# Modulation products spread through the projection steps' ring order in a two-block transformer kernel

## The reference

```python
c_act = jax.nn.silu(c)
for l in range(2):
    mod = c_act @ w_mod[l] + b_mod[l]            # 2048 x 6144
    shift, scale, gate = jnp.split(mod, 3, axis=-1)
    h = x * (1.0 + scale[:, None]) + shift[:, None]
    if l == 0:
        y = diff_attention(h, a_w_in, a_w_out, ...)
    else:
        mod_kv = c_act @ kv_w_mod + kv_b_mod      # 2048 x 4096
        k, v, F = shared_kv(x, ...)
        y = forgetting_attention(h, b_w_in, b_w_out, k, v, F)
    x = layer_norm(alpha * x + gate[:, None] * y, ln_g[l], ln_b[l])
# second block: adaln(c_2, w_mod_2) gives six vectors (2048 x 12288), then mixer, GLU, MLP
```

## Time and profile before

| what | value |
|---|---|
| median of 3 runs | 2741.72 us (2737.67 to 2751.97) |
| profiled execution, its own time | 2757.5 us |
| its span | 2755.6 us |
| PE busy | 2501.9 us, 91% |
| DVE busy | 1714.8 us, 62% |
| ACT busy | 1041.8 us, 38% |
| HBM traffic over the span | 255 GB/s |
| mean granted PE clock | 0.925 of full |

### The profile page before, as it was taken

How to read it: one execution, slowest core, us unless ns; L and a number is a source line. 1 busy time by engine, 2 the same in 40 slices (tenths; PEclk the granted TensorE clock), 3 DMA queues, 4 the chain that set the end, 5 groups by cost and what they waited for, 6 DMA issues and landing times.

```text
span 2755.6 us, 42740 instructions
## 1 busy us (share of the span) xinstructions
PE 2501.9 (91%) x18111; PEld 2059.6 (75%) x18111; DVE 1714.8 (62%) x2630; ACT 1041.8 (38%) x1556; POOL 177.4 (6%) x289
## 2 busy tenths in 40 slices
PE   5799999798789799989998958899899999999998
PEld 1588877566656598789854848578699898998986
DVE  4657789688767755356524755777755477655555
ACT  0253343344453333344423322344444444343443
POOL 1102233011100000111000000000000000000000
PEclk7799999899899899989977975999999999999999
DMA  9969999787678688969766748868645587755553
GB/s 353 337 219 356 349 336 313 234 294 288 244 260 308 244 286 308 353 209 312 258 220 218 249 90 309 327 232 276 236 133 189 183 274 276 244 184 191 188 171 107
DMA packets 317373, 699.74 MB, mean 254 GB/s; under 512 B 13600, under 2 KB 14080, under 8 KB 312192
## 3 DMA queue, kind: packets, MB, share of 16 engines
q1 hardware_dynamic: 298432, 627.27, 66.2%
q0 software_dynamic: 18480, 67.66, 7.0%
q10 hardware_dynamic: 272, 2.10, 0.2%
HBM read 646.77 MB, written 56.49 MB: 255 GB/s over the span
## 4 chain that ended last, share of the span: by engine, by line
PE 73%; DVE 15%; DMA 8%; ACT 2%; issue 1%; SPq 0%; POOL 0%; DVEq 0%; ACTq 0%; POOLq 0%
PE bank L2147 71%; DVE arena L1352 5%; DMA ring<-in_w_mod 3%; DMA ring<-in_a_w_in 3%; DVE ring_lo L1352 3%; DVE sm L1352 2%; DVE arena L1360 2%; PE bank L2150 1%; PE bank L2375 1%; DMA ring<-in_a_w_out 1%; DMA arena<-arena 0%; DVE MSB L1352 0%; DMA m_state<-MSB 0%; DVE LT L1360 0%; ACT att_w_hi L963 0%
## 5 line engine op out<-in xcount | busy, mean ns | idle before, releaser
L1352 DVE TENSOR_TENSOR ring_lo<-ring,w_hi 128x1024 fp32r<-128x1024 f32 (+1 forms) x380 | 427.7, 1134 | 359.9 <-ACT w_hi L963 334.8
L963 ACT CAST w_hi<-ring 128x1024 fp32r<-128x1024 f32 x316 | 330.6, 1049 | 472.5 <-PE bank L2147 470.4
L1352 DVE TENSOR_TENSOR ring_lo<-ring,att_w_hi 128x1024 fp32r<-128x1024 f32 x192 | 232.0, 1223 | 224.1 <-ACT att_w_hi L963 223.9
L963 ACT CAST att_w_hi<-ring 128x1024 fp32r<-128x1024 f32 x192 | 198.9, 1049 | 350.8 <-PE bank L2147 181.0
L2147 PE MATMUL bank<-in_hi,w_hi 128*128 128x256 f32 x1024 | 290.2, 283 | 1.2 <-DVE n L1357 1.2
L2147 PE MATMUL bank<-in_lo,w_hi 128*128 128x256 f32 x1024 | 290.1, 283 | 0.0
L2147 PE MATMUL bank<-in_hi,ring_lo 128*128 128x256 f32 x1024 | 289.7, 283 | 0.0
L2147 PE MATMUL bank<-w_hi,hid_lo 128*128 128x512 f32 x640 | 257.5, 402 | 5.2 <-DVE ring_lo L1352 5.2
L2147 PE MATMUL bank<-ring,cpad 128*32 128x512 f32 x1408 | 195.7, 691 | 26.1 <-DMA ring<-in_w_mod 22.5
L2147 PE MATMUL bank<-att_w_hi,att_hi 128*128 128x512 f32 x512 | 206.0, 402 | 6.9 <-DVE ring_lo L1352 6.9
L2147 PE MATMUL bank<-ring_lo,att_hi 128*128 128x512 f32 x512 | 202.7, 396 | 0.0
(11 more groups left out here) (259 smaller groups left out, 4998.5 us busy)
## 6 DMA issues: line engine op xcount, KB each, us to landing
ring<-in_w_mod SPq DMA_DIRECT2D x192, 1024.0 KB, 9.5
ring<-in_a_w_in SPq DMA_DIRECT2D x64, 1024.0 KB, 10.2
ring<-in_w_mlp_in SPq DMA_DIRECT2D x64, 1024.0 KB, 5.2
ring<-in_w_mlp_out SPq DMA_DIRECT2D x64, 1024.0 KB, 5.1
ring<-in_kv_w_mod SPq DMA_DIRECT2D x32, 1024.0 KB, 10.7
ring<-in_b_w_in SPq DMA_DIRECT2D x32, 1024.0 KB, 6.9
ring<-in_kv_w SPq DMA_DIRECT2D x32, 1024.0 KB, 5.6
ring<-in_s_w_glu SPq DMA_DIRECT2D x32, 1024.0 KB, 5.5
```

Source lines behind the costliest of these rows:

```text
L963: a.copy(whi(h), raw_half(h)).then_inc(*o.up("whi"))
L1352: return v.tensor_tensor(dst, x, y, op).then_inc(*(to or o.up("dve")))
```

## The change

A panel that PE takes is no longer behind its step but in it: in the ring its quarters lie each behind one chunk of the step, and PE takes a quarter after every second round (`mod_part`). `sums` of the panel before stands at the head of the next step that has a panel. Layer 0's attention has no panel any more (23 to 25 go to steps 0 to 2, 26 to step 3, 27 and 28 to the layer norm, 29 to 36 to steps 4 to 11), panel 37 goes to DVE, and DVE's four panels in steps 12 to 19 are 37 to 40; the last four pieces of 40 fall into the first four iterations of layer 1's attention, where the PE panels stand three iterations later. SP loads `proj_d[3]` only after the last write to `m_state` has landed.

```diff
--- before.py
+++ after.py
@@ -67,11 +67,10 @@
 
 MOD_AT_PRE = {**{pn: 8 + pn for pn in range(8)}, 9: 16, 11: 17}
 MOD_AT_BL = {0: 18, 9: 19, 10: 20, 19: 21, 20: 22}
-MOD_AT_A = {5: 23, 9: 24, 13: 25}
-MOD_AT_STEP = {0: 26, 1: 27, 2: 28, **{n: 26 + n for n in range(4, 12)}}
-MOD_AT_LN = (29,)
-
-MOD_AT_B = {2 + 5 * i: 41 + i for i in range(6)}
+MOD_AT_STEP = {**{n: 23 + n for n in range(4)}, **{n: 25 + n for n in range(4, 12)}}
+MOD_AT_LN = (27, 28)
+
+MOD_AT_B = {5 + 5 * i: 41 + i for i in range(6)}
 
 
 
@@ -89,11 +88,12 @@
 STEPS = FRONT + GLU + MLP
 N_Q, N_K, N_W1, N_GLU, N_MLP, NS = 4, 12, 20, len(FRONT), len(FRONT) + len(GLU), len(STEPS)
 
-DVE_MOD = {38: 12, 39: 14, 40: 16, 47: 20, 48: 24, 49: 26, 50: 28, 51: 30, 52: 40, 53: 42, 54: 44, 55: 46}
+DVE_MOD = {37: 12, 38: 14, 39: 16, 40: 18, 47: 20, 48: 24, 49: 26, 50: 28, 51: 30, 52: 40, 53: 42, 54: 44, 55: 46}
 DVE_NO = {j: i for i, j in enumerate(DVE_MOD)}
 
-SUMS_AT = {12: 37, 14: 38, 16: 39, 18: 40, 20: 46, 22: 47, 26: 48, 28: 49, 30: 50, 31: 51, 42: 52, 44: 53, 46: 54, 48: 55}
+SUMS_AT = {12: 36, 14: 37, 16: 38, 18: 39, 20: 46, 22: 47, 26: 48, 28: 49, 30: 50, 31: 51, 42: 52, 44: 53, 46: 54, 48: 55}
 DVE_PART = {(n + (c + 1) // 2, 2 - c % 2 * 2): (j, c) for j, n in DVE_MOD.items() for c in range(4)}
+DVE_PART[N_W1 - 1, 3] = DVE_PART.pop((N_W1, 0))
 
 ROW_AT = {N_GLU: "mix", NS - 6: "mlp"}
 TURNED = ("q", "k", "in")
@@ -133,8 +133,12 @@
             if (n, q) in DVE_PART:
                 ring.use(("mod", *DVE_PART[n, q]), slots)
             ring.use(("step", n, q), slots)
+            if n in MOD_AT_STEP:
+                ring.use(("mod", MOD_AT_STEP[n], q), slots)
         for b in range(2):
             bank.use(("step", n, b), GD)
+        if n in MOD_AT_STEP:
+            bank.use(("mod", MOD_AT_STEP[n]), GM)
 
     def tile(i):
         pn, k = divmod(i, 16)
@@ -187,8 +191,6 @@
             bank.use(("at", t - 4), GT)
         if t < 16:
             bank.use(("as", t), GL)
-        if t in MOD_AT_A:
-            mod(MOD_AT_A[t])
         if t >= 17:
             bank.use(("bc", "m0g", t - 17), GC)
     for layer in range(2):
@@ -204,8 +206,6 @@
             if n == N_K:
                 bank.use(("zf",), GC)
             step(n)
-            if n in MOD_AT_STEP:
-                mod(MOD_AT_STEP[n])
             if n == N_Q - 1:
                 for j in MOD_AT_LN:
                     mod(j)
@@ -394,8 +394,8 @@
                     "m2a": ("bm2", 0), "m2b": ("bm2", 0), "m2d": ("bm2", 0), "m2c": ("bm2", 0)}
 
         def mod_acc(j):
-            at = MSB if j > 47 else L2
-            return at[:, 512 * (DVE_NO[j] % 2):512 * (DVE_NO[j] % 2) + 512]
+            i = DVE_NO[j] % 2
+            return MSB[:, 512 * i:512 * i + 512] if j > 47 else (L2[:, 0:512], L1[:, 1536:2048])[i]
 
         def mod_base(j):
             return MOD_OFF[MOD_OF[MODS[j][0]]] + MODS[j][1]
@@ -657,6 +657,9 @@
                         j, c = DVE_PART[key[1], q]
                         load(("mod", j), MOD_W[MODS[j][0]], 0, 128 * MODS[j][1], c)
                     load(key, W, k0, n0, q)
+                    if key[0] == "step" and key[1] in MOD_AT_STEP:
+                        j = MOD_AT_STEP[key[1]]
+                        load(("mod", j), MOD_W[MODS[j][0]], 0, 128 * MODS[j][1], q)
 
             def mod(j):
                 load_w(("mod", j), MOD_W[MODS[j][0]], 0, 128 * MODS[j][1])
@@ -694,12 +697,10 @@
             sp.wait_ge(S["st1"], 16 * 11)
             sp.wait_ge(S["st2"], 16 * 10)
             sp.wait_ge(S["blm"], 32)
-            sp.dma_start(reg(4096, 4096), proj_d[3]).then_inc(S["p3"], 16)
 
             sp.wait_ge(S["ms0"], 16 * 16)
             sp.wait_ge(S["ms1"], 16 * 16)
-            for t in sorted(MOD_AT_A):
-                mod(MOD_AT_A[t])
+            sp.dma_start(reg(4096, 4096), proj_d[3]).then_inc(S["p3"], 16)
 
             W_OF = {"wout0": (A["a_w_out"][0], 0), "q": (A["b_w_in"][0], 0), "g": (A["b_w_in"][0], 2048), "k": (A["kv_w"], 0),
                     "v": (A["kv_w"], 2048), "wout1": (A["b_w_out"][0], 0), "value": (A["s5_w_glu_2"][0], 0),
@@ -1955,10 +1953,9 @@
 
             v.memset(ones, 1.0).then_inc(*o.up("ones"))
             for n in range(N_W1):
-                if n == N_Q - 1:
-                    mod_bias("m1s")
                 if n == N_Q:
                     layer_norm(0)
+                    mod_bias("m1s")
                     own()
                     ts(sc1, M("m1", 16), 1.0, None, ADD, None, *o.up("scol"))
                     split_in("q", h_raw["q"], sc1, M("m1", 0), AHk, ALk, N_Q, 8 * n)
@@ -1984,7 +1981,7 @@
                 round_of(n, n in (N_Q - 1, N_W1 - 1))
                 if n == N_K - 2:
                     mod_bias("kv")
-                elif n == N_K + 4:
+                elif n == N_K + 6:
                     mod_bias("m1g")
             v.wait_ge(*filled("nFT"))
             ts(nFT[0:16, :], bank("nFT")[0:16, 0:256], -1.0, None, MUL, None, *empty("nFT"))
@@ -2013,6 +2010,8 @@
                     stt(p, bank("fs", i)[:, 0:w_], FN[:, t2, h:h + 1], negm[:, t2, 0:w_], ADD, ADD, *empty("fs", i))
                     own()
                     v.tensor_reduce(s_[:, 0:1], p, AX, MAX, negate=True).then_inc(*o.up("fmax"))
+                if t < 4:
+                    mod_piece(N_W1 - 1, 4 + t)
 
             for h in range(8 * N_W1, 8 * N_W1 + 4):
                 w_lo(h)
@@ -2181,13 +2180,16 @@
                 if j and j - 1 != MOD_END["m0s"] and j - 1 not in SUMS_AT.values():
                     sums(j - 1)
                 for q in range(4):
-                    w = chunk("mod", j, q)
-                    p.wait_ge(*landed("mod", j, q))
-                    if q == 0:
-                        room("mod", j)
-                    for i in range(4):
-                        t = mm(bank("mod", j)[32 * i:32 * i + 32, :], cwide[:, 4 * q + i, :], w[:, i, :], q == 0, q == 3)
-                    t.then_inc(*(fill("mod", j) if q == 3 else (S["taken"], 1)))
+                    mod_part(j, q)
+
+            def mod_part(j, q):
+                w = chunk("mod", j, q)
+                p.wait_ge(*landed("mod", j, q))
+                if q == 0:
+                    room("mod", j)
+                for i in range(4):
+                    t = mm(bank("mod", j)[32 * i:32 * i + 32, :], cwide[:, 4 * q + i, :], w[:, i, :], q == 0, q == 3)
+                t.then_inc(*(fill("mod", j) if q == 3 else (S["taken"], 1)))
 
             def turn_scaled():
 
@@ -2240,6 +2242,8 @@
             def multiply(n):
                 kind, gr, pn = STEPS[n]
                 a_hi, a_lo = (AHk, ALk) if n < N_GLU else (DHk, DLk) if kind == "out" else (HHk, HLk)
+                if n in MOD_AT_STEP and MOD_AT_STEP[n] - 1 not in SUMS_AT.values():
+                    sums(MOD_AT_STEP[n] - 1)
                 for j in range(2):
                     room("step", n, j)
                 for r in range(8):
@@ -2277,6 +2281,8 @@
                                 t.then_inc(*fill("step", n, j))
                     if r < 7:
                         t.then_inc(S["half"], 1)
+                    if r % 2 and n in MOD_AT_STEP:
+                        mod_part(MOD_AT_STEP[n], r // 2)
 
             def pre_tile(i):
 
@@ -2463,8 +2469,7 @@
                         t = mm(bank("as", t_)[:, 256 * c:256 * c + w_], qT[0][:, 2 * h + c, 128 * t2:128 * t2 + 128],
                                kT[0][:, 2 * h + c, 0:w_], True, True)
                     t.then_inc(*fill("as", t_))
-                if t_ in MOD_AT_A:
-                    mod(MOD_AT_A[t_])
+
                 if t_ >= 17:
                     bcast("m0g", M("m0", 32), t_ - 17)
 
```

## The result

The changed kernel takes **2774.34 us** (median of 4, 2772.19 to 2775.78) against 2742.39 for the kernel before (2737.67 to 2751.97) on the same chip: ratio 1.0111, 95% interval 1.0083 to 1.0140. Forecast were 2750 us and at most 2767. It is 32 us slower, not 8.

What follows compares the result with a forecast made beforehand. PE was taken to bound steps 1 to 11, a chain through two transfers layer 0's attention. Terms summed to -2.1 us, plus 10.2 for the clock: +8.1 us, put on the median 2741.72: 2750 us, range 2732 to 2767.

Steps and rivals of the forecast that it cites:

- The new wait at each step's end: At ten step ends in steps 0 to 10, PE's sums wait for ACT's copy of the panel's bank: +14.6 us.
- rival 3: The chunk ahead of `finish` lands late, some 3 us more at five step ends: 2765 us; chance 0.05.
- The clock: PE's granted clock falls after the quiet stretch at six of ten step ends, 1.7 us each: +10.2 us.
- Steps 0 to 3 and 4 to 11: In each of the two stretches PE gets 0.75 panel more on its path: +2.7 us each.
- Attention without panels and the moved load: Layer 0's attention: DVE's idle times at three panels go, -12.3 us; last `m_state` write lands earlier, -5.0 us.
- Ahead of step 12: After step 11, DVE starts on the `k` operand 3.5 us after the step's end, not 10.1: -6.5 us.
- Layer norm: Behind step 3, two panels instead of one fit into PE's idle time: cost 0, up to 3 us without that cover.
- steps 18, 19 with layer 1's attention: DVE's last four pieces cost 1.3 us in layer 1's attention, `sums(40)` moved there 1.4: +2.7 us.
- Clock holds: Rival: the waits at the step ends come, but no fall of the clock follows: 2740 us; chance 0.14.
- All ten: Rival: the clock falls at all ten step ends, 17 us: 2757 us; chance 0.17.
- Cold attention: Rival: layer 0's attention runs at the lower clock without the panels' wide matmuls, 18 us more: 2768 us; chance 0.06.
- Warmer elsewhere: Rival: PE runs at full clock before steps 4 and 12 and in layer 1's attention, -20 us: 2720 us; chance 0.10.

Runs made afterwards that it cites:

- filler: The changed kernel with 4, 5 or 9 useless wide matmuls in PE's wait for ACT's copy at step ends: 2759.22 us, 1.0064 of the kernel before.
- base: The kernel before, unchanged, run and profiled once more: 2747.1 us, ratio 1.0006; its profiled execution took 2754.1 us.
- late: The changed kernel with the sums moved from the step's head to after its second round: 2743.9 us, 0.9981 of the kernel before.
- burst: The changed kernel's placement of panels, but each panel whole and behind its step, in the ring too: 2750.57 us, 1.0009 of the kernel before.
- p3: The kernel before with only the load of `proj_d[3]` moved behind the last write to `m_state`: 2748.21 us, 1.0008 of the kernel before.
- half: `late` with panels in two halves, after the fourth and eighth rounds, in the ring too: 2731.83 us, 0.9961 of the kernel before.

## Why the prediction was wrong, point by point

**What failed** is the sum, in one term that is absent and in where it was put; the mechanism that was named as the costly one is right.

- **The new wait at each step's end, +14.6: right.** 17.8 us in all, 16.4 of it at the ten step ends. The waits of `q` and `g` were 1.11 to 1.28 (1.4 forecast), that at step 8's end, with the table load, 2.37 (2.7), those of steps 1 and 2 0.71 (1.15). Nine waits were shorter than forecast; the excess is one of 5.52 at step 0's end: the late chunk of rival 3, at one end and not five. The layer norm's sums waited 0.71 twice, in time that PE has there anyway.
- **The clock, +10.2: right.** Seven falls, not six. Taking each as its length times what its granted clock lacks of full, they come to 1.3 to 1.9 us each, 11 in all; holding the clock at six of them in `filler` made those steps 10.3 us shorter. It held behind the two waits of 0.71, fell behind that of 5.52, and behind those of 1.11 to 2.37 fell six times in seven. The count is in part luck: the prediction took 2.88 us of idle time for a sure fall and set six of ten between it and 1.18, but behind the same 2.88 us the clock held in `base` and in the changed kernel. The Trainium skill, TensorE: Matmul & The Clock Gate (section HAM oscillation), has every following burst throttled by a wait that recurs at every tile, in its case a wait of some 3 to 5 us; here, with nine waits of 0.7 to 2.4 us and one of 5.5, it was seven of ten, with a recovery after each.
- **The turns: absent.** The prediction counted moved panels by their busy time, 3.64 us for a whole one and 0.91 for a quarter, and charged nothing for going from a step's matmuls to a panel's and back four times. At 0.33 us a turn, three more in each of twelve steps are 12 us; the sums standing alone add 0.16 a step (from one step's sums to the next in step 7 it is 29.77 us, less the wait of 1.19 28.6, in `late` 28.4): some 12 to 14 us in all. This is the step that failed. The row that could have told it is in the trace of before: behind a panel the first matmul takes 0.39 us instead of 0.28, and the second starts 0.22 after it, not 0.12. Busy times can't show it, since PE is "busy" in it.
- **Steps 0 to 3 and 4 to 11, +2.7 each:** the 0.75 panels are there, in either. With these, 5.4, less the 1.2 of the idle time after step 0, the ten waits 16.4, the clock 11, the turns 12 and the gain ahead of step 12, 7.1, the sum is 36.5, and 34 to 37 were measured between step 0 and step 12.
- **Attention without panels and the moved load, -17.3 together:** from 700 to step 0 the traces gain 15 to 16 us, of which the moved load is about 3 (DVE's idle time 14.9 and 14.1 before, 11.57 after), not 5. The write lands after 7.8 us, not 6. The Trainium skill, DMA: Bandwidth & Descriptors (section Queues, rings and completion order), lets the queues take turns by the packet; by that rule alone one load fewer would have gained nothing, and 11.2 against 7.1 and 7.8 us speaks against that; but `burst`, with one load fewer and 9.7 us, shows that the number of loads is not the whole reason. The rest is open.
- **Ahead of step 12, -6.5: right.** DVE starts on `k` 3.0 us after step 11's end (10.1 before), -7.1.
- **Layer norm, 0, and steps 18, 19 with layer 1's attention, +2.7:** the first is right within 1.3 us. From where the transposes for `k` begin to step 20's first matmul it is 330.5 us in the changed kernel, against 330.7 and 334.7 in the two long traces of the kernel before and 322.8 in `p3`. So the second is nothing to -4 us by the former and +8 by the latter; what two traces of one kernel differ by hides it.
- **The number.** The sum was made against a trace 15 us above its median and then put on the median. In its own frame it was +8.1 where the traces differ by 15.9 (19.3 against `base`): 8 to 11 short, about the turns. The other 13 to 16 us of the miss are the step from trace to median. It took for granted that the excess of the one trace would be absent from the changed kernel's median; but the eight executions of the changed kernel all lie between 2770.6 and 2775.8. The traces show where such an excess can lie: from step 12 to the end it is 1566 and 1570 us in the two long traces of the kernel before, 1570.7 in the changed kernel, and 1556.5 in `p3`, whose trace is near its median and whose code is the same there as before. Where the two forms part is seen: mostly in layer 1's attention, at the six panels. Their matmuls in `p3` and in `base`, from the view of the tile `cpad`:

```profile
L2147 PE MATMUL bank<-ring,cpad x192: 592/606/1062, 1393.8 to 1483.2; 128*32 128x512 f32 x192
L2147 PE MATMUL bank<-ring,cpad x192: 592/1058/1063, 1387.5 to 1489.3; 128*32 128x512 f32 x192
```

The middle number is the median in ns: in `p3` most run at full clock, in `base` most at half, and 11.9 of the 13.6 us between the two traces lie between step 12 and step 20. Both traces of the changed kernel have the longer form (1570.7 and 1569.9), as have `late` (1570.3) and `burst` (1568.7); `filler` (1562.5) and `half` (1563.7) have the shorter. Why the changed kernel has the long form in both of its traces was not found; it is open.
- **The rivals.** Clock holds: false. All ten: false, seven. Late chunk: at one end. Cold attention: false, 0.97 in the window, above the 0.92 of before. Warmer elsewhere: false. None of the rivals had the turns, and the range, 2732 to 2767, was too narrow by them: each of its terms came from an idle time or a busy time.

## What to carry to other kernels

Interleaving small pieces of one kind of matmul into another costs PE at each turn, and no idle time shows it: measure from the start of the last matmul ahead to the start of the second behind, and take the largest piece that does not bring late loads or late copies (of those tried here, halves were the fastest). A short operation whose input another engine has just begun to make is to be placed a round later, not at the seam: that was worth some 24 us between step 0 and step 12 for two lines, 16 of it the waits themselves, most of the rest the clock. Before putting a sum on a median, take a second profile of the same kernel; and before giving an experiment's whole difference to its edit, see in which stage it lies.

## What the hardware showed that was not expected

- A turn between the step's matmuls (`fp32r`, 256 or 512 columns) and the panel's float32 ones of 32 columns cost 0.33 us, with no idle time of PE in it.
- PE was busy in 3.5 us windows near the lower clock after only 1.11 us of idle time and 1.05 us of one-column matmuls (0.55 at 974.0); after 0.71 and 1.05 it stayed at full. After 1.11 and 1.05 it stayed once too (1036.6), and after an idle 2.88 us it stayed in `base` and fell in `late`, so the idle time alone does not tell. A fall cost 1.3 to 1.9 us by the windows and 1.3 to 2.1 by the steps.
- Matmuls whose results are thrown away, in a wait of about one microsecond, kept the clock at full at six step ends more and made the steps behind them 10 us shorter in all.
- Ten executions of one kernel on one chip spread over 17 us, broadly in step with their mean granted clock (0.925 to 0.934); the eight of the changed kernel spread over 5 us only. Why the change makes the times steadier stays open.
- Within one kernel the six panels in layer 1's attention ran mostly at full clock in one trace and mostly at half in another (medians 606 and 1058 ns), worth up to 12 us.
